# Decay products of the linear attention on GpSimd, and PSUM banks emptied ahead of the weight split in even slots

## The chip, the cores and the metric

One core of one Trainium2 chip runs the whole program in one launch. The metric is device microseconds (us), median over the runs; the kernel before was run three times.

## The reference, cut to what matters

Two blocks of a model run one after the other on 256 tokens of width 1024, all in float32. The change lies in the second block, which has two layers. Each layer is a feed-forward, a token mixer with two branches, and a feed-forward. The branches are a sparse attention of 8 heads and a gated linear attention (4 heads, key width 128, value width 256). Of the linear attention this is computed:

```python
q_dec = qc * jnp.exp(b)
k_intra = kc * jnp.exp(-b)
k_state = kc * jnp.exp(b_last - b)
A = jnp.where(causal, jnp.einsum('bnihd,bnjhd->bnhij', q_dec, k_intra), 0.0)
o_intra = jnp.einsum('bnhij,bnjhv->bnihv', A, vc.astype(jnp.float32))
```

Here b is the running sum of the logarithm of a gate. The branches then go through two output products, each scaled by a sigmoid gate of a projection of the same input.

## The kernel before, in words

**Split products.** All large products are made in a format with fewer mantissa bits, so each weight chunk (128 x 2048 float32, a ring of 4 slots loaded from HBM by SyncE's queue) is split in two parts. ScalarE writes the high part of a chunk (`mix_split`, L1552 to L1563, two halves of 128 x 1024), VectorE the low part (`mix_low`, L2287 to L2295, two halves, each after ScalarE's half). TensorE then makes three matmuls of 512 columns for each 128 x 128 weight block. A ring slot comes free when TensorE has read it, and its load is issued then.

**The attention part of a layer.** `attention()` exists once for each engine (TensorE L1267, ScalarE L1907, VectorE L2807), and the engines keep step by semaphores alone. The sparse attention goes over four pairs of heads, j = 0 to 3. Round j has these steps:
- TensorE: scores of the pair (L1277 to L1284), then `side_pair` (L1162), the product of one half of a projection with its weights, 48 matmuls of 128x512 into the two banks `side`. Then the transposes of the probabilities (`turn`, L1294, L1296), a second `side_pair`, and the values (L1309 to L1315).
- VectorE: maxima of the pair (L2824, L2827), the probabilities' scale (L2834 to L2841), the slot `beside(2j)`, two PSUM copies of transposed probabilities for each head (`turned`, L2848 and L2849), the slot `beside(2j+1)`, and, once ScalarE has taken its high part, the low part of the output (`output_low`, L2934) ahead of the next maxima.
- ScalarE: exponentials of the pair (L1912), `beside(2j)`, its share of the copies (L1920, L1921), `beside(2j+1)`, and the high part of the output (L1925).

**The slots.** `beside(s)`, s = 0 to 7 (ScalarE L1966, VectorE L2908), carries the projections that are made beside the heads. In slot s, ScalarE splits the chunks 16+2s and 17+2s, which the *next* `side_pair` reads (the first in its first half, the second in its second half), and empties the two `side` banks that the *current* `side_pair` fills (`side_take`, L1885, recorded at L1890). Slots 0 and 1 carry the values, 2 and 3 the output gate (two copies from each bank), 4 and 5 the first merge gate, 6 and 7 the second. From slot 2 on, the taking of the second bank is followed by `sigmoid_rest` (L1946 to L1950): a logarithm and an exponential over 128x1024, each with its table load.

The linear attention's own steps stand in the same slots. VectorE does the absolute value in slot 0 (L2910), the running sums in slot 2 (`sums`, L2851 to L2858), the differences in slot 3 (L2865), the gate product in slot 4 (L2923, L2924). ScalarE forms the decays in slot 4 (`decays`, L1932 to L1940). In slot 5 VectorE multiplies decays with queries and keys (`operands`, L2868 to L2878: four products of 128x512, two of 128x1024) and clears the 128x2048 tile `PlL` of weights (L2928). In round 3 TensorE makes the far weights (`far_weights`, L1224) between the first `side_pair` and the transposes, in the same two `side` banks, and the near weights (`near_weights`, L1241) after the second `side_pair`. VectorE collects both into `PlL` (`collect_far` L2880, `collect_near` L2895).

**GpSimd** masks weights in the first block (L3106), issues a few DMAs (L3110 to L3119), and then waits for the end of the last layer's attention to issue one more (L3122). Its queue is in order.

Of the kernel before, what the change touches and what calls it, by code (L numbers as in the profile page):

```python
# [9 lines left out]
ALU = mybir.AluOpType  # L10
# [3 lines left out]
P = 128  # L14
# [18 lines left out]
def build(nc, t, out):  # L33
    ctx = ExitStack()
    with ctx:
# [3 lines left out]
        def sem(name):  # L39
            return ctx.enter_context(nc.semaphore(name))  # L40
# [311 lines left out]
        gl_d = sem("gla_differences")  # L352
        gl_e = sem("gla_decays")
        gl_g = sem("gla_operands")
        gl_o = sem("gla_values")
        rb_done = sem("gla_gate_done")
        rb_sig = sem("gla_gate_sigmoid")
# [1048 lines left out]
        def _(act):  # L1406
# [500 lines left out]
            def attention():  # L1907
# [58 lines left out]
                def beside(s):  # L1966
                    l = c.layer - 1
                    if s == 6:
                        act.wait_ge(rb_done, c.layer)
                    for i in range(2):  # L1970
                        n = 2 * (s % 2) + i
                        mix_split(l, 16 + 2 * s + i)
                        if s < 2:
                            values(n)
                        elif s < 4:
                            gate(n)
                        elif s < 6:
                            merge_gate_(n, y2, gm_sig)
                        else:
                            merge_gate_(n, r2, gm1_sig)  # L1980
                    if s == 1:
                        log_decays()
                    elif s == 4:
                        decays()
                    if s in (6, 7):
                        c.side += 2 if s == 6 else 1
# [107 lines left out]
        def _(dve):  # L2094
# [685 lines left out]
            def side_give(fn):  # L2780

                dve.wait_ge(side_full, c.side + 1)
                fn(side[c.side % 2]).then_inc(side_out[c.side % 2], 1)
                c.side += 1
# [22 lines left out]
            def attention(l):  # L2807
# [57 lines left out]
                        dve.tensor_tensor(out=o, in0=v.rearrange("p h (n w) -> p h n w", w=per), in1=ref,  # L2865
                                          op=ALU.subtract).then_inc(gl_d, 1)

                def operands():  # L2868
                    for u in range(2):
                        dve.wait_ge(gl_e, 3 * c.layer - 2 + u)  # L2870
                        for half, src in enumerate((khL, qhL)):
                            o, s_ = (v.rearrange("p h (n a b) -> p h n a b", a=2, b=P >> u)[:, :, :, half, :]
                                     for v in (dec[:, u, :, :], src))
                            ins = dve.tensor_tensor(out=o, in0=s_, in1=o, op=ALU.mult)
                        ins.then_inc(gl_g, 1)
                    dve.wait_ge(gl_e, 3 * c.layer)
                    dve.tensor_tensor(out=dek, in0=khL, in1=dek, op=ALU.mult)
                    dve.tensor_tensor(out=dec[:, 2, :, :], in0=qhL, in1=dec[:, 2, :, :], op=ALU.mult).then_inc(gl_g, 1)  # L2878

                def collect_far():  # L2880
                    def across(b):
                        return dve.tensor_copy(PlL[:, :, 0, P:S], b[:, :].rearrange("p (h b) -> p h b", b=P))

                    def within(b):
                        for st in range(2):
                            ins = dve.tensor_copy(PlL[0:64, :, st, st * P + 64:st * P + P],
                                                  b[0:64, st * S:(st + 1) * S].rearrange("p (h b) -> p h b", b=64))
                        return ins

                    side_give(across)  # L2890
                    side_give(within)
                    dve.wait_ge(side_out[(c.side - 1) % 2], (c.side - 1) // 2 + 1)
                    dve.wait_ge(side_out[c.side % 2], c.side // 2)
# [14 lines left out]
                def beside(s):  # L2908
# [8 lines left out]
                    if s == 2:  # L2917
                        sums()
                    elif s == 3:
                        differences()  # L2920
                    elif s == 4:
                        dve.wait_ge(rb_sig, 2 * c.layer)
                        step(dve.tensor_tensor(out=rx, in0=rx, in1=r2, op=ALU.mult))  # L2923
                        dve.tensor_tensor(out=rx, in0=rx, in1=gainC.unsqueeze(1).to_broadcast([P, 2, D]),  # L2924
                                          op=ALU.mult).then_inc(rb_done, 1)
                    elif s == 5:
                        operands()
                        step(dve.memset(PlL[:, :, :, :], 0.0))  # L2928
                    elif s == 7:
                        collect_near()  # L2930

# [165 lines left out]
        def _(gp):  # L3097
            c = Count()

            for h in range(H):  # L3100
                for d in range(2):
                    gp.wait_ge(p_done, 2 * h + d + 1)
                    for n in range(2):
# [2 lines left out]
                        ins = gp.affine_select(out=v, in_=v, compare_op=ALU.is_ge, fill=0.0, base=0,  # L3106
                                               pattern=[[sign, P]], channel_multiplier=-sign)
                    ins.then_inc(pm_done, 1)
            gp.wait_ge(resid, 12)
            gp.dma_start(gateB[:, 1, :], t["fgain"][0:1].to_broadcast([P, D])).then_inc(final_in, 16)  # L3110
            gp.dma_start(onehot, t["onehot"]).then_inc(bias_dma, 16)
# [6 lines left out]

            gp.dma_start(TB, bass.AP(t["scratch"].tensor, P - 1, [[H * RW - 1, P], [RW, H], [1, S]])).then_inc(  # L3119
                bias_done, 16)  # L3120
            gp.wait_ge(hn_out, 2)
            gp.dma_start(gainC, t["fgain"][1:2].to_broadcast([P, D])).then_inc(final_in, 16)  # L3122
            gp.wait_ge(stored, 64)
# [179 lines left out]
```

## Time and profile before

| | |
|---|---|
| median of 3 runs | 2425.76 us (2425.75 to 2430.88) |
| profiled execution, its own time | 2424.43 us |
| its span in the profile | 2422.7 us |
| TensorE busy, share of the span | 2351.5 us, 97% |
| VectorE / ScalarE / GpSimd busy | 1570.5 / 1162.6 / 13.0 us |
| mean granted TensorE clock | 0.994 of full |
| attention of the first layer of block two | about 1405 to 1529 us of the span |
| attention of the second layer | about 2041 to 2165 us of the span |

In a timeline row the first number is the start in us from the span's start, the second the time of the group in us; [x <- engine tile line] is how long the engine sat idle before it and who ended that.

### The profile page before, as it was taken

What the parts mean: (1) busy time and instruction counts of PE and PEld (TensorE: products, weight loads), DVE (VectorE), ACT (ScalarE), POOL (GpSimd) and SP (SyncE); (2) the same over time, 40 slices, a digit from 0 to 9 for tenths busy, and PEclk for the clock granted to TensorE, in tenths of its full rate; (3) what the DMA queues carried; (4) which work ended last, traced back from release to release, by engine and by line L of the source; (5) the groups of instructions that cost most, each with busy time, mean ns of one, the idle gap of its engine ahead of it and who ended that gap; (6) DMA issues with size and microseconds to landing.
All of it is one profiled execution on the core that took longest, in us unless ns stands there. A gap on an engine that the chain in (4) does not pass through costs nothing.

```text
span 2422.7 us, 33029 instructions
## 1 busy us (share of the span) xinstructions
PE 2351.5 (97%) x13342; PEld 1974.8 (82%) x13342; DVE 1570.5 (65%) x2355; ACT 1162.6 (48%) x1725; POOL 13.0 (1%) x43
## 2 busy tenths in 40 slices
PE   7999999999999999999999998999999999989998
PEld 4887787888888887888888887888888888878887
DVE  4686434656655686667766468676776665766766
ACT  4212323435533345445444478554454446874444
POOL 0000000000000000000000000000000000000000
PEclk9999999999999999999999999999999999999999
DMA  7467322323521224654455643345545555434553
GB/s 301 188 240 267 122 91 103 120 87 124 203 86 57 88 90 164 235 191 174 175 190 191 221 157 140 134 180 191 190 175 191 191 171 217 152 119 164 195 189 137
DMA packets 57920, 399.67 MB, mean 165 GB/s; under 512 B 7789, under 2 KB 8309, under 8 KB 10280
## 3 DMA queue, kind: packets, MB, share of 16 engines
q1 hardware_dynamic: 52704, 383.80, 43.4%
q10 hardware_dynamic: 4272, 10.08, 1.2%
q0 software_dynamic: 800, 3.73, 0.5%
q8 instruction: 106, 1.74, 0.3%
q14 instruction: 38, 0.31, 0.0%
HBM read 396.53 MB, written 2.63 MB: 165 GB/s over the span
## 4 chain that ended last, share of the span: by engine, by line
PE 85%; DVE 6%; ACT 6%; DMA 1%; issue 1%; SPq 0%; DVEq 0%; ACTq 0%
PE pair L506 80%; DMA ring<-in_stream 1%; DVE ring_parts L2294 1%; ACT mix_high L1562 1%; PE pair L901 1%; DVE ring_parts L2284 1%; ACT arena L1912 1%; PE pair L619 1%; PE pair L884 1%; PE pair L1039 1%; ACT ring_high L1549 1%; PE pair L1294 0%; PE pair L848 0%; DVE rows L2411 0%; DVE X L2417 0%
## 5 line engine op out<-in xcount | busy, mean ns | idle before, releaser
L506 PE MATMUL pair<-xT_parts,ring_high 128*128 128x512 f32 x2112 | 747.8, 395 | 4.2 <-DVE ring_parts L2284 1.1
L506 PE MATMUL pair<-xT_parts,ring_parts 128*128 128x256 f32 (+2 forms) x2448 | 694.6, 298 | 7.4 <-DVE ring_parts L2294 4.9
L2284 DVE TENSOR_TENSOR ring_parts<-ring,ring_high 128x2048 fp32r<-128x2048 f32 x194 | 444.1, 2292 | 142.1 <-ACT ring_high L1549 142.0
L506 PEld LDWEIGHTS pair<-xT_parts,ring_parts 128*128 128x128 f32 (+1 forms) x2448 | 461.5, 189 | 51.2 <-issue 12.1
L506 PEld LDWEIGHTS pair<-xT_parts,ring_high 128*128 128x128 f32 x2112 | 384.5, 188 | 81.8 <-DVE ring_parts L2284 2.7
L1549 ACT ACTIVATE ring_high<-ring 128x2048 fp32r<-128x2048 f32 x198 | 377.3, 1909 | 68.2 <-DMA ring<-in_stream 68.2
L2294 DVE TENSOR_TENSOR ring_parts<-ring,mix_high 128x1024 fp32r<-128x1024 f32 x144 | 168.5, 1219 | 77.6 <-ACT mix_high L1562 77.2
L1600 ACT ACTIVATE arena<-pair 128x512 f32<-128x512 f32 x110 | 65.5, 596 | 259.7 <-PE pair L506 259.6
L506 PE MATMUL pair<-ring_parts,xT_parts 128*128 128x512 f32 (+1 forms) x448 | 174.3, 389 | 0.2 <-DVE rows L2524 0.2
L1562 ACT ACTIVATE mix_high<-ring 128x1024 fp32r<-128x1024 f32 x144 | 143.1, 1047 | 61.6 <-DMA ring<-in_stream 57.7
L506 PE MATMUL pair<-ring_parts,g_high 128*128 128x512 f32 x440 | 171.8, 391 | 0.2 <-issue 0.2
L506 PE MATMUL pair<-ring_high,g_high 128*128 128x512 f32 x440 | 171.3, 389 | 0.0
L506 PE MATMUL pair<-ring_high,g_low 128*128 128x512 f32 x440 | 171.2, 389 | 0.0
L506 PE MATMUL pair<-mix_high,xT_parts 128*128 128x512 f32 (+1 forms) x576 | 171.0, 380 | 0.0
L2337 DVE TENSOR_TENSOR arena<-pair,arena 128x512 f32<-128x512 f32 x110 | 75.7, 689 | 96.6 <-ACT arena L1600 96.6
L506 PE MATMUL pair<-xT_low_parts,ring_high 128*128 128x512 f32 x352 | 137.0, 389 | 0.0
L1562 ACT ACTIVATE grid_weights<-ring 128x1024 fp32r<-128x1024 f32 x56 | 56.1, 1052 | 140.6 <-PE pair L506 127.8
L506 PEld LDWEIGHTS pair<-mix_high,xT_parts 128*128 128x128 f32 x576 | 106.3, 188 | 20.5
L1611 ACT ACTIVATE arena<-arena 128x256 f32<-128x256 f32 x110 | 46.0, 418 | 141.2 <-DVE arena L2345 123.2
L1593 ACT ACTIVATE arena<-pair 128x512 f32<-128x512 f32 x22 | 13.1, 598 | 187.4 <-PE pair L506 187.4
L506 PE MATMUL pair<-xT_parts,mix_high 128*128 128x256 f32 (+1 forms) x544 | 100.7, 287 | 0.0
L506 PEld LDWEIGHTS pair<-ring_parts,xT_parts 128*128 128x128 f32 x448 | 84.1, 188 | 19.1 <-issue 2.3
(417 smaller groups left out, 3908.2 us busy)
## 6 DMA issues: line engine op xcount, KB each, us to landing
ring<-in_stream SPq DMA_DIRECT2D x338, 1024.0 KB, 4.8
xn<-in_mods SPq DMA_DIRECT2D x14, 1024.0 KB, 4.9
arena<-in_mods SPq DMA_DIRECT2D x14, 1024.0 KB, 4.9
arena<-in_bT ACTq DMA_DIRECT2D x1, 1536.0 KB, 8.9
bias_scratch<-bias_row POOLq DMA_DIRECT2D x1, 1536.0 KB, 8.3
X<-in_x ACTq DMA_DIRECT2D x1, 1024.0 KB, 11.9
X<-in_ctx ACTq DMA_DIRECT2D x1, 1024.0 KB, 16.4
arena<-in_bT ACTq DMA_DIRECT2D x1, 1024.0 KB, 7.3
```

What stands on the lines that cost most here:

```text
L506: m = pe.matmul(o, l, r, start=start, stop=stop)
L619: m = pe.matmul(bank[k][:, t_ * P:(t_ + 1) * P], X[:, t_, k * P:(k + 1) * P], diag[:, t_, :], start=True, stop=True)
L884: pe.matmul(bank[n // 2][:, (n % 2) * S:(n % 2 + 1) * S], km[lo:lo + 64, h // 2, n * P:(n + 1) * P], qm[lo:lo + 64, h // 2, :], start=True ...
L901: m = pe.matmul(misc[d][:, tt * 129:(tt + 1) * 129], Pm[d][:, n, tt * P:(tt + 1) * P], va[:, n, h, :], start=n == keys[0], stop=n == keys[-1])
L1039: m = pe.matmul(acc[c.acc % 4][:, st * S:(st + 1) * S], KX[d][:, 1, hh, st * P:(st + 1) * P], QP[d][:, hh, :], start=d == 0, stop=d == 1)
L1549: act.activation(high[:, ch % SLOTS, :], ring[:, ch % SLOTS].rearrange("p a b -> p (a b)"), ACT.Copy).then_inc(high_ready, 1)
L1562: act.activation(mix_high(l, m)[:, half], ring[:, ch % SLOTS].rearrange("p a b -> p (a b)")[:, half], ACT.Copy).then_inc(mix_high_ready, 1)
L1600: act.activation(cross[:, f % 2, :, :], pair[f % 2][:, :, S:2 * S], ACT.Copy).then_inc(cross_done, 1)
L1611: act.activation(sil2[:, f % 2, :], both[:, f % 2, 0, :], ACT.Silu).then_inc(sil_done, 1)
L2284: dve.tensor_tensor(out=ring_r[:, slot].rearrange("p a b -> p (a b)"), in0=w, in1=high[:, slot, :], op=ALU.subtract).then_inc(low_ready, 1)
L2294: dve.tensor_tensor(out=ring_r[:, slot].rearrange("p a b -> p (a b)")[:, half], in0=w, in1=mix_high(l, m)[:, half], op=ALU.subtract).then_ ...
L2337: dve.tensor_tensor(out=both[:, f % 2, :, :], in0=pair[f % 2][:, :, 0:S], in1=cross[:, f % 2, :, :], op=ALU.add).then_inc(both_done, 1)
```

## The change

Three things change, in both layers. `operands` goes from VectorE's slot 5 to GpSimd, with the same waits on ScalarE's decays. The clearing of `PlL` goes with it, behind the wait for the last decays, and VectorE's `collect_far` waits for it by a new semaphore. In ScalarE's even slots the split of each of the two chunks comes after the taking of the bank of the same index, and so, in slots 2, 4 and 6, the second chunk's split comes after `sigmoid_rest` too. Odd slots stay as they were.

```diff
@@ ScalarE, beside(s) @@
                     for i in range(2):
                         n = 2 * (s % 2) + i
-                        mix_split(l, 16 + 2 * s + i)
+                        if s % 2:
+                            mix_split(l, 16 + 2 * s + i)
                         if s < 2:
                             values(n)
...
                         else:
                             merge_gate_(n, r2, gm1_sig)
+                        if s % 2 == 0:
+                            mix_split(l, 16 + 2 * s + i)
@@ VectorE @@
-                def operands():
...
+                    dve.wait_ge(far_clear, c.layer)
                     side_give(across)
...
-                    elif s == 5:
-                        operands()
-                        step(dve.memset(PlL[:, :, :, :], 0.0))
@@ GpSimd @@
+            def operands(l):
+
+                for u in range(2):
+                    gp.wait_ge(gl_e, 3 * l + u + 1)
+                    for half, src in enumerate((khL, qhL)):
+                        o, s_ = (v.rearrange("p h (n a b) -> p h n a b", a=2, b=P >> u)[:, :, :, half, :]
+                                 for v in (dec[:, u, :, :], src))
+                        ins = gp.tensor_tensor(out=o, in0=s_, in1=o, op=ALU.mult)
+                    ins.then_inc(gl_g, 1)
+                gp.wait_ge(gl_e, 3 * l + 3)
+                gp.memset(PlL[:, :, :, :], 0.0).then_inc(far_clear, 1)
+                gp.tensor_tensor(out=dek, in0=khL, in1=dek, op=ALU.mult)
+                gp.tensor_tensor(out=dec[:, 2, :, :], in0=qhL, in1=dec[:, 2, :, :], op=ALU.mult).then_inc(gl_g, 1)
...
                 bias_done, 16)
+            operands(0)
+            operands(1)
             gp.wait_ge(hn_out, 2)
```

## Rows read from the trace of the kernel before

**Rows 1.** Page, part 1: busy us (share of the span) x instructions.
```profile
PE 2351.5 (97%) x13342; PEld 1974.8 (82%) x13342; DVE 1570.5 (65%) x2355; ACT 1162.6 (48%) x1725; POOL 13.0 (1%) x43
```

**Rows 2.** Waits of TensorE: who for whom, us in total, times, longest.
```profile
PE pair L506 <- ACT arena L1890: 12.9, 4, 6.1
```

**Rows 3.** Timeline, TensorE, round 3 of the first layer.
```profile
1508.59 2.04 PE L506 MATMUL pair<-arena 128*128 128x128 f32 x8 [6.12 <-ACT arena L1890]
1510.96 1.94 PE L506 MATMUL pair<-arena 128*64 128x64 f32 x16 [0.33 <-ACT arena L1890]
...
1525.92 1.15 PE L506 MATMUL pair<-arena 128*64 128x64 f32 x32
```

**Rows 4.** Timeline, ScalarE, slot 6.
```profile
1501.31 0.40 ACT L1912 ACTIVATE arena<-arena 128x128 f32<-128x128 f32 x1 [4.76 <-DVE arena L2827]
...
1505.98 1.99 ACT L1562 ACTIVATE mix_high<-ring 128x1024 fp32r<-128x1024 f32 x2
1507.87 0.57 ACT L1890 ACTIVATE arena<-pair 128x512 f32<-128x512 f32 x1
```

**Rows 5.** Timeline, VectorE, end of slot 5.
```profile
1492.43 2.49 DVE L2874 TENSOR_TENSOR arena<-arena 128x512 f32<-128x512 f32 x4
...
1497.56 1.76 DVE L2928 MEMSET arena<- 128x2048 f32 x1 [0.38 <-issue]
1499.36 0.43 DVE L2934 TENSOR_TENSOR oaT_low<-pair,oaT_high 128x256 fp32r<-128x256 f32 x1
```

**Rows 6.** Timeline, ScalarE, slot 2: second split, sigmoid, then copies.
```profile
1445.00 2.00 ACT L1562 ACTIVATE mix_high<-ring 128x1024 fp32r<-128x1024 f32 x2
...
1447.98 1.28 ACT L1949 ACT_TABLE_LOAD   x1
...
1452.61 0.47 ACT L1920 ACTIVATE arena<-pair 128x384 f32<-128x384 f32 x1
```

**Rows 7.** Timeline, VectorE, slots 2 to 4.
```profile
1444.24 4.63 DVE L2294 TENSOR_TENSOR ring_parts<-ring,mix_high 128x1024 fp32r<-128x1024 f32 x4
1448.78 1.22 DVE L2853 SCALAR_TENSOR_TENSOR arena<-arena 128x1024 f32<-128x1024 f32 x1
...
1454.74 2.36 DVE L2294 TENSOR_TENSOR ring_parts<-ring,mix_high 128x1024 fp32r<-128x1024 f32 x2
...
1465.55 0.42 DVE L2934 TENSOR_TENSOR oaT_low<-pair,oaT_high 128x256 fp32r<-128x256 f32 x1 [1.17 <-ACT oaT_high L1925]
...
1478.80 2.29 DVE L2923 TENSOR_TENSOR gateB<-gateB,arena 128x2048 f32<-128x2048 f32 x1
```

**Rows 8.** Timeline, TensorE: start of a side product, and the values of two rounds.
```profile
1448.09 0.48 PE L506 MATMUL pair<-ring_parts,xT_parts 128*128 128x512 f32 x1
...
1459.16 1.08 PE L1309 MATMUL pair<-arena 128*64 128x256 f32 x8
...
1487.12 1.08 PE L1309 MATMUL pair<-arena 128*64 128x256 f32 x8
```

**Rows 9.** Timelines of GpSimd and VectorE in the first block, GpSimd's last DMA.
```profile
502.16 0.54 POOL L3106 TENSOR_SCALAR_AFFINE_SELECT arena<-arena 128x128 f32<-128x128 f32 x2 [0.59 <-DVE arena L2487]
...
2177.36 0.55 POOL L3122 DMA_DIRECT2D gateB<-in_fgain  x1 [1190.74 <-DVE xn L3019]
...
502.42 2.48 DVE L2294 TENSOR_TENSOR ring_parts<-ring,first_high 128x1024 fp32r<-128x1024 f32 x2 [0.33 <-ACT first_high L1562]
...
552.64 2.36 DVE L2294 TENSOR_TENSOR ring_parts<-ring,first_high 128x1024 fp32r<-128x1024 f32 x2 [0.45 <-ACT first_high L1562]
```

**Rows 10.** TensorE timeline (two stalls); then windows, PEclk the number ahead of DMA share.
```profile
705.45 0.74 PE L506 MATMUL pair<-arena 128*64 128x64 f32 x17 [1.88 <-DVE arena L2689]
...
1385.18 0.38 PE L506 MATMUL pair<-xT_parts,ring_parts 128*128 128x256 f32 x1 [1.40 <-DVE ring_parts L2294]
...
705.50:707.50 2.00, 2.00 (x69) 2.00 (x71) 1.58 (x2) 1.62 (x2) 0.00 (x0) 1.00 0.45 57
...
1388.50:1389.00 0.50, 0.50 (x4) 0.50 (x3) 0.50 (x2) 0.50 (x1) 0.00 (x0) 0.50 0.86 360
```

More of the change, by code:

```diff
@@ L354, in build @@
         gl_g = sem("gla_operands")
+        far_clear = sem("gla_weights_cleared")
         gl_o = sem("gla_values")
@@ L2866, in differences @@
                                           op=ALU.subtract).then_inc(gl_d, 1)
-                def operands():
[L2869 to L2878, printed above, removed]
                 def collect_far():
```

## The prediction

> **What bounds the kernel now.** The page first: TensorE is busy for 97% of the span [rows 1], so a change on the other engines can only pay where TensorE stands still. The waits of TensorE show one such place that this change touches: `L506 <- ACT L1890`, four waits, 12.9 us in all, the longest 6.1 [rows 2]. The timeline has two of them in round 3 of each layer: before the first far weights (6.12 us) and before the second (0.33 us) [rows 3]. The layers are alike to 0.1 us, so I work out the first and count it twice.
>
> TensorE waits there for a `side` bank that ScalarE empties at 1507.87, after a split that began at 1505.98 [rows 4]. ScalarE itself had stood idle for 4.76 us before its exponentials at 1501.31, waiting for VectorE's maxima [rows 4]. VectorE was late because the products and the clearing held it from 1492.43 to 1499.36, 6.93 us [rows 5]. So the chain is products, clearing, maxima, exponentials, split, bank, and both parts of the change aim at it.
>
> The gap has a second price. The far weights ran slowly, as at the half clock that [rows 10] show after another stall: the second group, 16 matmuls, took 1.94 us, while 32 of the same kind later took 1.15 us [rows 3]. At full clock 16 would take 0.6, so 1.3 us a layer could come back.
>
> **Part 1, VectorE's relief in slot 5.** 6.93 us of VectorE go away, but not all is gained: the next step, `output_low`, waits for ScalarE's high part, and ScalarE was busy until 1501.31 - 4.76 = 1496.55. From there VectorE needs 1.95 us for the low part and one head's maxima (1499.36 [rows 5] to 1501.31 [rows 4]), which sets the exponentials at 1498.5 instead of 1501.3: 2.8 us.
>
> **Part 2, slot 6.** The bank is taken where the split began, 1.89 us earlier [rows 4]; the second bank gains the same. Parts 1 and 2 at this place alone would be 4.7, and with the clock 6.0 us a layer.
>
> **Part 3, the same edit in slots 2 and 4.** The diff moves the second chunk's split behind `sigmoid_rest` as well. That takes from 1447.98 to 1452.61, 4.63 us [rows 6]. Slot 2, step by step. Before, the second split began at 1445.00 [rows 6]. Now ScalarE's exponentials end at 1442.15 (1445.00 less a split of 1.9 and a bank of 0.95), it waits 1.5 for TensorE to fill bank 0, takes it (1.0), splits (1.9), takes bank 1 (1.0) and does the sigmoid (4.65). The second chunk's first half is out at about 1453.15, its low part 1.15 later, at 1454.3. TensorE's next side product began at 1448.09 and reads that chunk 5.5 us later [rows 8], at 1453.6: it stalls 0.7. VectorE, in order, is done with the slot's low parts at 1455.5, not 1448.8 [rows 7]; the sums and PSUM copies queued behind took from 1448.78 to 1454.74 [rows 7], 5.8 without idle time, and follow to 1461.2. TensorE's values, at 1459.16 before [rows 8] and 1459.9 now, wait for those copies: 1.3 more. Slot 3's splits and differences are done 5.0 us later; 1.17 of it was idle there [rows 7], so the next maxima, and ScalarE's exponentials, start 3.9 us later.
>
> Slot 4 repeats this on top: TensorE loses 0.9 at the transposes and the chunk's first use, 1.0 at its second chunk, and 1.5 at the copies, since VectorE's gate product (twice 2.29) [rows 7] again stands between late low parts and copies (values at 1492.6; 1487.12 before [rows 8]). TensorE arrives at round 3 5.5 us late, which eats most of the 6.45 us gap. ScalarE's output part is 4.0 late, at 1500.2. By then VectorE, without the products, is through (1497.2) and waits, so the exponentials start at 1502.1 (before: 1501.3). Bank 1 is taken, by the new order, at 1509.8, where the second far product before began at 1510.96 [rows 3]. TensorE ends its side product at 1507.8, does the first far product at full clock, and the second is done at 1510.3 instead of 1512.3 by the same bookkeeping: a gain of 2.0 us a layer, 4.0 in all. Slot 0 costs nothing: VectorE's absolute value covers the later split. Slot 6's late second split is covered too: TensorE reads that chunk 5.5 us into a side product that starts at 1512.
>
> **Part 4, GpSimd's work.** No row shows its two-input product. From below I take VectorE's own rate (0.62 us for each of the four, 2.49 / 4 [rows 5]), from above twice the select's rate: 0.27 us for 128 columns [rows 9] gives 1.1 us for 512 columns and one input, 2.2 for two. I take 1.1 and, for 1024 columns, 2.2, nearer to the low end because part of a select is fixed cost. The clearing lies between VectorE's 1.76 [rows 5] and 16 selects, 4.3 us. The six products and the clearing then take 11 us from 1486.4 on: the first far product is fed at 1489 and needed at 1508, the near one at 1497 and 1524. At twice the durations this still holds, so GpSimd's speed is on no path, nor is the new wait of `collect_far`. Behind the waiting GpSimd stands one DMA, at 2177.36, which waits for the last attention anyway [rows 9]. SyncE's loads follow TensorE's reads as before.
>
> **What the products do to VectorE** is the open price. In the first block a VectorE subtraction of the chunk kind overlapped a GpSimd select once: the pair took 2.48 us against 2.36 elsewhere, 0.12 more for some 0.27 of GpSimd [rows 9]. Bounds: nothing, or all of GpSimd's time in turns. I take the row: VectorE loses 0.45 of GpSimd's busy time where both read two operands. The first four products (4.4 us) fall on the gate product and stretch it and what follows by 2.3 us. The copies and values come that much later, TensorE reaches the far weights at 1510.1, after ScalarE; of the gain of 2.0 only 0.7 is left.
>
> The stall at the copies is then 3.8 us. Short stalls can cost clock: one of 1.40 us at 1385.18 was followed by windows with a granted clock of 0.50, while one of 1.88 us at 705.45 was followed by 1.00 [rows 10]. The drop after the first lasted 3.5 us, so 1.75 us of work; I charge it once a layer. Result: -0.7 + 1.8 = +1.1 us a layer, +2.2 in all. Against the profiled execution (2424.43) that is 2426.6; the median shown is 1.3 above it, so 2428.0.
>
> **Rivals.**
> - **No contention** (the bound of nothing). -2.0 a layer, 2421.8; with a drop of the clock after the stalls of 1.3 to 1.5 us, near 2425. For it: a select is a poor stand-in, the overlap is one row. Against: the row is not zero. Chance 0.21.
> - **VectorE and GpSimd take turns by whole instructions** (slower). The gate product and slot 5's four low parts stand against the six products: while GpSimd reads two operands, a VectorE instruction of two SBUF operands does not run. Each such instruction waits for a product of 1.1 or 2.2 us: together 7.8 us by 1505, so maxima start 4.8 us after the no-contention schedule, ScalarE is last again, the gap opens by 2 us and the clock falls before the far weights (1.3). -2.0 + 4.8 + 1.3 = +4.1 a layer, 2434.0. It decides once VectorE loses more than about two thirds of GpSimd's time. For it: 0.12 us is all that the select's reading of 128 columns can hold. Against: the select's full 0.27 was not lost. Chance 0.31. The Trainium skill, page "SBUF — State Buffer", section "Who interferes with whom", says that a VectorE instruction with two SBUF inputs contends with a GpSimd instruction that reads SBUF, and that the pair of ports is locked for a whole instruction; by it the sum would be this one.
> - **The order costs nothing in slots 2 and 4**, and the full 6.0 us a layer come: 2413.8. That asks that TensorE not miss the late chunk halves, which its own rows contradict. Chance 0.11.
> - The forecast, stretched or not by the clock (-1 to +2.4 a layer: 2424 to 2430.6), has 0.37.
>
> **Numbers.** 0.2% is 4.9 us, about what a measurement of this kernel can tell from no change. Forecast and no contention lie within it, but for 0.05 of the latter's and 0.05 of the former's chance at either side. Faster 0.16, same 0.48, slower 0.36. The range leaves out the full gain and the upper part of the turns (GpSimd's products longer still): 2420 to 2437.
>
> **What would show it.** In the changed profile: idle before the first far weights down from 6.12 to under 1 us (turns: 2 or more); new TensorE waits on L2294 in slots 2 and 4 of 0.5 to 1 us and on the copies before L1309 of 1.3, then 1.5 to 4 us; the gate product L2923 and L2924 at 2.29 us (no contention), 3 or more (forecast), or stretched by whole products (turns); GpSimd's products at 1.1 and 2.2 us; granted clock under 1.00 after the copies' stall. If TensorE has no new waits before round 3, part 3 is wrong and the time is near 2414.

## The result and the profile after

The changed kernel takes 2433.99 us (median of 11 runs, 2429.52 to 2437.81), the kernel before beside it 2427.82 us (11 runs, 2425.75 to 2430.88). The ratio is 1.0025, 95% interval 1.0016 to 1.0033: slower by 6.2 us. The time lies in the forecast range, 6.0 us above the 2428.0 us forecast; 2.1 of these 6.0 us lie in the kernel before, which took 2425.76 us in the three runs that the forecast started from. So a forecast of +2.2 stands against a measured +6.2 us. The profiled execution took 2430.51 us, span 2428.2, and is the second fastest of the eleven, so its trace shows less than the median loses.

The engines' busy times, page part 1, answer to [rows 1]:

```profile
PE 2355.7 (97%) x13342; PEld 1975.1 (81%) x13342; DVE 1566.1 (64%) x2341; ACT 1163.9 (48%) x1725; POOL 54.0 (2%) x57
```

VectorE lost 14 instructions but only 4.4 us, though 6.93 us a layer of products and clearing had left it. GpSimd is busy 41.0 us longer, where 11 us a layer had been costed. A good part of both numbers is waiting for each other.

Waits of TensorE (who for whom, us in total, times, longest), then its timeline in the first layer. They answer to [rows 2, 3]:

```profile
PE pair L1310 <- DVE arena L2853: 9.3, 4, 3.4
...
PE pair L507 <- DVE ring_parts L2298: 8.9, 11, 1.4
```

```profile
1458.05 0.50 PE L507 MATMUL pair<-ring_parts,xT_parts 128*128 128x512 f32 x1 [1.07 <-DVE ring_parts L2298]
...
1465.05 1.08 PE L1310 MATMUL pair<-arena 128*64 128x256 f32 x8 [1.22 <-DVE arena L2853]
...
1481.62 0.88 PE L1295 MATMUL pair<-ident,arena 128*128 128x128 f32 x6 [0.32 <-DVE arena L2845]
...
1489.34 0.50 PE L507 MATMUL pair<-ring_parts,xT_parts 128*128 128x512 f32 x1 [0.80 <-DVE ring_parts L2298]
...
1498.51 1.97 PE L1310 MATMUL pair<-arena 128*64 128x256 f32 x8 [3.43 <-DVE arena L2853]
...
1516.86 2.13 PE L507 MATMUL pair<-arena 128*128 128x128 f32 x24
```

The wait for `side` banks, 12.9 us before, is gone: the far weights start without idle time, all 24 matmuls in 2.13 us. In its place stand the five waits for VectorE shown above, in slots 2 and 4. They add up to 6.84 us in this layer, where before there were 6.45. Idle time was moved, not removed. The values at 1498.51 took 1.97 us where the same eight matmuls took 1.08 before [rows 8]: they ran at the lower clock.

Time, busy time and clock by round, TensorE first (PEclk is the number ahead of the DMA share). A round goes from the values of one pair to the values of the next. First the kernel before, first layer, rounds 1 to 3:

```profile
1431.21:1459.16 27.95, 27.95 (x157) 22.42 (x156) 21.69 (x68) 26.16 (x52) 0.00 (x0) 1.00 0.43 151
1459.16:1487.12 27.96, 27.96 (x158) 22.43 (x157) 22.80 (x64) 25.86 (x53) 0.00 (x0) 1.00 0.40 151
1487.12:1526.90 39.78, 33.34 (x214) 27.16 (x214) 30.15 (x75) 29.87 (x56) 0.00 (x0) 0.91 0.29 106
```

Then the changed kernel, with round 0 ahead:

```profile
1405.53:1434.40 28.87, 28.87 (x136) 23.97 (x137) 20.44 (x65) 15.32 (x40) 0.00 (x0) 0.88 0.40 146
1434.40:1465.05 30.65, 28.36 (x157) 22.38 (x157) 19.11 (x66) 27.59 (x54) 0.00 (x0) 1.00 0.38 138
1465.05:1498.51 33.46, 28.79 (x157) 22.39 (x157) 27.62 (x67) 28.75 (x56) 8.41 (x4) 1.00 0.35 126
1498.51:1532.71 34.20, 34.20 (x212) 27.19 (x214) 25.00 (x68) 25.96 (x51) 11.98 (x4) 0.90 0.33 124
```

Rounds 1 and 2 are 2.70 and 5.50 us longer, round 3 is 5.58 us shorter. Of the 8.20 us only 6.96 are idle time. The other 1.24 us stand in TensorE's busy time at a clock of 1.00 (28.36 + 28.79 against 27.95 + 27.96); by an estimate from these numbers each of the five stalls costs a further 0.25 us beyond its idle time. Round 0 is no part of the change: its 28.87 against 25.8 us elsewhere is a drop of the clock that falls there in some executions of several of these kernels. I therefore read rounds 1 to 3 alone, both layers together: 191.1 us before, 195.0 after, +4.0. This sum is the yardstick below.

VectorE in the changed kernel, from slot 4's low parts to the maxima, answers to [rows 5, 7]:

```profile
1488.07 2.36 DVE L2298 TENSOR_TENSOR ring_parts<-ring,mix_high 128x1024 fp32r<-128x1024 f32 x2 [4.23 <-ACT mix_high L1563]
1490.34 3.39 DVE L2916 TENSOR_TENSOR gateB<-gateB,arena 128x2048 f32<-128x2048 f32 x1
1493.77 3.28 DVE L2917 TENSOR_TENSOR gateB<-gateB 128x2048 f32<-128x2048 f32 x1
...
1498.29 4.61 DVE L2298 TENSOR_TENSOR ring_parts<-ring,mix_high 128x1024 fp32r<-128x1024 f32 x4
1503.80 0.42 DVE L2924 TENSOR_TENSOR oaT_low<-pair,oaT_high 128x256 fp32r<-128x256 f32 x1 [0.90 <-ACT oaT_high L1926]
...
1507.24 0.92 DVE L2831 TENSOR_SCALAR arena<-arena 128x6 f32<-128x6 f32 x1
```

GpSimd in the same stretch, and the eight 128x512 products by themselves (ns, least, median, greatest):

```profile
1490.10 13.93 POOL L3107 TENSOR_TENSOR arena<-arena 128x512 f32<-128x512 f32 x4 [501.53 <-ACT arena L1938]
1503.98 1.80 POOL L3110 MEMSET arena<- 128x2048 f32 x1
1505.74 2.39 POOL L3111 TENSOR_TENSOR arena<-arena 128x1024 f32<-128x1024 f32 x1
```

```profile
L3107 POOL TENSOR_TENSOR arena<-arena x8: 1477/3330/5911, 1490.1 to 2134.9; 128x512 f32<-128x512 f32 x8
```

The gate product was 2.29 and is 3.39 and 3.28. The four small products are 1.48, 3.34, 3.32 and 5.90 us long in order. The lengths fit VectorE and GpSimd waiting for each other's whole instructions: the first gate instruction has 1.10 us more in its record, the time until the first product was over, and the second product waited for it (3.34 = some 2.1 of waiting and 1.2 of work). The fourth product then waited for all of slot 5's low parts, which were themselves not stretched (4.61 for four). The clearing takes 1.80 to 1.82 us in all these kernels.

### The profile page after: what moved, and what is told of

It reads as the page before. It is cut to its first block, busy times and chain, and to the rows that moved or that the text cites. A ratio compares the mean times of both kernels' runs of the same rounds, so it can differ in the third digit from the quotient of the medians.

```text
span 2428.2 us, 33029 instructions
## 1 busy us (share of the span) xinstructions
PE 2355.7 (97%) x13342; PEld 1975.1 (81%) x13342; DVE 1566.1 (64%) x2341; ACT 1163.9 (48%) x1725; POOL 54.0 (2%) x57
## 4 chain that ended last, share of the span: by engine, by line
PE 85%; DVE 7%; ACT 5%; DMA 2%; issue 1%; SPq 0%; DVEq 0%; ACTq 0%
PE pair L507 80%; DVE ring_parts L2298 2%; DMA ring<-in_stream 2%; DVE ring_parts L2288 1%; PE pair L902 1%; ACT mix_high L1563 1%; ACT ring_high L1550 1%; PE pair L885 1%; PE pair L1040 1%; ACT arena L1913 0%; DVE rows L2415 0%; PE pair L620 0%; DVE X L2421 0%; PE pair L849 0%; PE pair L1280 0%
## 6 DMA issues: line engine op xcount, KB each, us to landing
X<-in_x ACTq DMA_DIRECT2D x1, 1024.0 KB, 12.1
```

## The experiments

Theory A: the late split behind `sigmoid_rest` in slots 2 and 4 costs more than the rest of the change gains, and contention of GpSimd with VectorE and the clock after the long stall are smaller terms on top. The rivals: GpSimd's contention is the loss; or the order's loss is small and the gain never was there. The table sums up all kernels. "Rounds" is the yardstick against the kernel before (191.1), "idle" TensorE's idle time in rounds 1 to 3 of the first layer (window less busy time), "work" its busy time in round 3 there.

| kernel | median, us | its kernel before | ratio, 95% interval | rounds, us | idle, us | work in round 3 |
|---|---|---|---|---|---|---|
| before | | | | 0 | 6.4 | 33.3 |
| the change | 2433.99 | 2427.82 | 1.0016 to 1.0033 | +4.0 | 7.0 | 34.2 |
| e1_gp_only | 2424.20 | 2428.81 | 0.9975 to 0.9994 | -2.8 | 4.2 | 34.2 |
| e2_order_only | 2434.59 | 2428.81 | 1.0014 to 1.0033 | +9.6 | 9.4 | 34.0 |
| e3_gp_slot6 | 2422.92 | 2428.81 | 0.9966 to 0.9988 | -5.1 | 3.0 | 34.0 |
| e4_split_before_sigmoid | 2424.45 | 2428.81 | 0.9978 to 0.9996 | -5.4 | 2.9 | 32.6 |
| e5_near_on_vector | 2421.67 | 2428.69 | 0.9959 to 0.9981 | -8.1 | 2.7 | 32.8 |
| e11_near_again (same) | 2421.58 | 2429.01 | 0.9956 to 0.9981 | -8.4 | 2.7 | 32.7 |
| e6_clear_and_slot6 | 2423.65 | 2428.69 | 0.9970 to 0.9988 | -4.6 | 3.3 | 34.1 |
| e7_after_gate_first | 2428.98 | 2428.69 | 0.9991 to 1.0010 | -0.2 | 6.9 | 31.3 |
| e8_low_parts_apart | 2434.46, one run | 2428.69 | | +5.7 | 7.1 | 32.7 |
| e9_slot6_only | 2428.58 | 2429.01 | 0.9990 to 1.0007 | -2.3 | 4.6 | 34.3 |
| e12_slot6_again (same) | 2424.77 | 2428.01 | 0.9981 to 0.9998 | -2.1 | 4.6 | 33.9 |
| e10_after_low_parts | 2423.66 | 2429.01 | 0.9973 to 0.9991 | -5.6 | 3.0 | 32.8 |

The yardstick comes from one execution each and agrees with the difference of the medians within 2.2 us, except for e2 (3.8 us), whose profiled execution was itself 4.5 us above its median.

**GpSimd's part alone** (all of the change but ScalarE's order):

```diff
@@ ScalarE, beside(s): as before the change @@
-                        if s % 2:
-                            mix_split(l, 16 + 2 * s + i)
+                        mix_split(l, 16 + 2 * s + i)
...
-                        if s % 2 == 0:
-                            mix_split(l, 16 + 2 * s + i)
```

> GpSimd forms the products and clears the weights; ScalarE's slots are as in the kernel before. Theory A (the order in slots 2 and 4 is what costs; GpSimd's share of the contention is small): no TensorE wait in slots 2 and 4, the wait before the first far weights falls from 6.1 to about 3 us, the way from a layer's first scores to its last values is about 117 us (before: 121.5 and 121.2), the time is 7 to 9 us below the kernel before. Theory B (GpSimd beside VectorE is what costs): the gate product L2916 and L2917 stays stretched and VectorE is late, the time is above that of the kernel before by 2 us or more.

**The order alone** (the four lines above as in the change; products and clearing stay on VectorE):

```diff
@@ VectorE, against the change @@
+                def operands():
...
-                    dve.wait_ge(far_clear, c.layer)
...
+                    elif s == 5:
+                        operands()
+                        step(dve.memset(PlL[:, :, :, :], 0.0))
@@ GpSimd @@
...
-            operands(0)
-            operands(1)
```

> ScalarE's even slots take the banks first, as in the changed kernel; products and clearing stay on VectorE. Theory A: TensorE waits about 0.7 to 1.1 us at the late chunk halves and 1.3 to 1.5 us at the copies in slots 2 and 4, and since VectorE's 6.9 us come on top, the wait before the far weights is still 3 us or more: 122 to 125 us from scores to last values, time 3 to 8 us above the kernel before. Theory B: the order costs nothing and saves up to 2 us a layer: time 2 to 6 us below the kernel before.

Measured: the first 4.6 us faster than before, less than the 7 to 9 expected; the second 5.8 us slower, as expected. TensorE's two stalls in round 3 with GpSimd's part alone, and VectorE's slot 5:

```profile
1511.66 2.05 PE L507 MATMUL pair<-arena 128*128 128x128 f32 x8 [3.90 <-ACT arena L1891]
1514.04 1.94 PE L507 MATMUL pair<-arena 128*64 128x64 f32 x16 [0.33 <-ACT arena L1891]
```

```profile
1493.07 9.45 DVE L2295 TENSOR_TENSOR ring_parts<-ring,mix_high 128x1024 fp32r<-128x1024 f32 x4 [3.05 <-ACT mix_high L1563]
```

TensorE with the order alone, slot 4:

```profile
1492.59 0.50 PE L506 MATMUL pair<-ring_parts,xT_parts 128*128 128x512 f32 x1 [0.79 <-DVE ring_parts L2297]
...
1499.67 1.08 PE L1309 MATMUL pair<-arena 128*64 128x256 f32 x8 [1.34 <-DVE arena L2852]
```

The whole loss of the change is there without GpSimd, and the new stalls 1.07, 1.27, 0.31 and 0.79 are those of the changed kernel to 0.05 us. The last one, before the values, is 1.34 without GpSimd and 3.43 with it. GpSimd's part alone is a gain, but VectorE's slot 5 shows its price: the four low parts take 9.45 us instead of 4.6, since here they meet the 128x1024 products. So the gap closes by 2.2 us, not by 2.8.

**The order in slot 6 only, and the split ahead of the sigmoid.**

```diff
@@ e3_gp_slot6, against the change @@
-                        if s % 2:
+                        if s != 6:
                             mix_split(l, 16 + 2 * s + i)
...
-                        if s % 2 == 0:
+                        if s == 6:
                             mix_split(l, 16 + 2 * s + i)
@@ e4_split_before_sigmoid: all even slots, but inside the taking of the bank @@
                     side_take((dst[:, t_, g * N:(g + 1) * N], lambda b: b[:, :], ACT.Exp, -1.0))
+                    if split_m is not None:
+                        mix_split(c.layer - 1, split_m)
                     if t_:
...
```

> The changed kernel, but the bank is taken ahead of the split in slot 6 alone; slots 0, 2 and 4 have the old order. Theory A: no waits in slots 2 and 4, the wait before the first far weights about 1 us and before the second about 1.5 us, 114.5 us from scores to last values, time 11 to 14 us below the kernel before. Theory B: as the changed kernel, 4 us or more above the kernel before.

> The changed kernel, but in the even slots the second chunk's split stands between the taking of the second bank and the logarithm and exponential of the sigmoid. Theory A, which lays the cost on the split that waits 4.6 us behind the sigmoid and not on the bank being taken first: TensorE has no waits in slots 2 and 4, about 1.5 us are left before each far product, 115.2 us from scores to last values, time 10 to 13 us below the kernel before. Rival to it: taking the banks first costs by itself (a split 1 us later is late enough): time at or above the kernel before.

Measured: 5.9 and 4.4 us faster than before. Almost no waits are left in slots 2 and 4, as expected, but the gains expected, 11 to 14 and 10 to 13 us, were about twice as large or more. Round 3 still runs in part at the lower clock (0.91 in e3; 0.95 and 0.91 in e4). TensorE in e3:

```profile
1507.72 1.34 PE L507 MATMUL pair<-arena 128*128 128x128 f32 x8 [1.99 <-ACT arena L1891]
1510.10 1.94 PE L507 MATMUL pair<-arena 128*64 128x64 f32 x16 [1.04 <-ACT arena L1891]
```

The change differs from e3 in slots 0, 2 and 4 of ScalarE's order alone, and is 12.1 us slower (+6.2 against -5.9, each to its own kernel before). e4 says that it is not the early bank that costs but the 4.6 us of sigmoid between the bank and the second split: with the split ahead of it, the stalls of slots 2 and 4 fall from 6.84 to 0.2 us and the gain stands.

**Which part of GpSimd's work gains.**

```diff
@@ e5_near_on_vector, against e3: the two 128x1024 products stay on VectorE @@
...
+                    elif s == 5:
+                        dve.wait_ge(gl_e, 3 * c.layer)
+                        dve.tensor_tensor(out=dek, in0=khL, in1=dek, op=ALU.mult)
+                        dve.tensor_tensor(out=dec[:, 2, :, :], in0=qhL, in1=dec[:, 2, :, :], op=ALU.mult).then_inc(gl_n, 1)
...
@@ e6_clear_and_slot6, against e3: GpSimd only clears, VectorE's operands() as before @@
...
             def operands(l):
-                for u in range(2):
...
                 gp.wait_ge(gl_e, 3 * l + 3)
                 gp.memset(PlL[:, :, :, :], 0.0).then_inc(far_clear, 1)
-                gp.tensor_tensor(out=dek, in0=khL, in1=dek, op=ALU.mult)
...
@@ e10_after_low_parts, against e3 @@
             def operands(l):
+                gp.wait_ge(mix_low_ready, 2 * split_before(l, 27) + 2)
```

> GpSimd forms only the four products of 128x512 and clears the far weights; the two products of 128x1024 stay on VectorE at the end of slot 5, as before; ScalarE's early take of the first bank stands in slot 6 alone (as in e3). Theory A (the two products of 128x1024 on GpSimd take turns with slot 5's low parts and stretch them to 9.4 us, and this delays the maxima and the exponentials of slot 6): slot 5's four low parts together fall to 4.6 to 5.1 us, TensorE's idle time before the first far weights falls from 1.99 to about 1.0 us, and the time lies 1 to 2 us under e3, so 7 to 9 us under the kernel before. Rival (the stretch of the low parts lies beside other work, and what the products cost on VectorE comes back): the same as e3 within 1 us, with the gap before the first far weights at 2 us or more.

> All six decay products stay on VectorE; GpSimd only clears the far weights (1.8 us); ScalarE's early take of the first bank stands in slot 6 alone. Theory A (the move of the products to GpSimd is worth almost nothing net: it frees 5 us of VectorE and gives most of it back in stretched low parts): as fast as e3 within 2 us, 5 to 8 us under the kernel before, with slot 5's low parts at 4.6 to 5.1 us and no stretch of the gate product. Rival (the products' move is what gained in e1 and e3): 3 us or more above e3, so at most 3 us under the kernel before, with a gap of 3 us or more before the first far weights.

> As e3 (products and clearing on GpSimd, ScalarE's order changed in slot 6 alone), but GpSimd starts only when VectorE has finished slot 5's low parts. Theory A (GpSimd's products cost VectorE only where its instructions read two operands from SBUF, and only these turns stretch it): slot 5's four low parts take 4.6 to 5.1 us, the products of 128x512 about 1.3 us each, TensorE's gap before the first far weights is 1.0 to 1.6 us, and the time equals that of e5 (7 us under the kernel before) within 2 us. Rival (the later start makes the products themselves late, or they take turns with the maxima as well): the far product waits for the products or the maxima are 2 us or more late, and the time is at or above that of e3 (6 us under the kernel before).

> The same kernel as e5_near_on_vector, beside the two others of this group. If its lead over e3 and e6 was more than the drops of the clock that wander between executions, it is again 6 to 8 us under the kernel before and 1 to 3 us under the other two here.

Measured: e5 and its repeat e11 7.0 and 7.4 us faster than before, e6 5.0, e10 5.4. The gap before the far weights in e5 is 1.48 us where about 1.0 was expected. Against the kernels measured beside it, e11 is 2.1 us under e10 and 7.0 under e9_slot6_only (below). TensorE and VectorE in e5:

```profile
1509.77 1.13 PE L508 MATMUL pair<-arena 128*128 128x128 f32 x8 [1.48 <-ACT arena L1892]
1512.15 1.94 PE L508 MATMUL pair<-arena 128*64 128x64 f32 x16 [1.25 <-ACT arena L1892]
```

```profile
1493.62 5.03 DVE L2299 TENSOR_TENSOR ring_parts<-ring,mix_high 128x1024 fp32r<-128x1024 f32 x4 [3.06 <-ACT mix_high L1564]
```

VectorE in e10, where GpSimd's clearing and its products of 128x1024 meet the maxima, then GpSimd, ScalarE and TensorE there:

```profile
1501.84 1.08 DVE L2831 TENSOR_SCALAR arena<-arena 128x6 f32<-128x6 f32 x1
...
1503.33 1.96 DVE L2831 TENSOR_SCALAR arena<-arena 128x6 f32<-128x6 f32 x1
...
1505.44 2.16 DVE L2838 TENSOR_SCALAR arena<-arena 128x6 f32<-128x6 f32 x1 [0.15 <-ACT arena L1913]
```

```profile
1501.09 1.81 POOL L3111 MEMSET arena<- 128x2048 f32 x1
1502.86 2.39 POOL L3112 TENSOR_TENSOR arena<-arena 128x1024 f32<-128x1024 f32 x1
1505.21 2.36 POOL L3113 TENSOR_TENSOR arena<-arena 128x1024 f32<-128x1024 f32 x1
```

```profile
1502.96 0.41 ACT L1913 ACTIVATE arena<-arena 128x128 f32<-128x128 f32 x1 [2.90 <-DVE arena L2831]
```

```profile
1508.38 1.79 PE L507 MATMUL pair<-arena 128*128 128x128 f32 x8 [2.43 <-ACT arena L1891]
```

Clearing plus slot 6 (e6) gets 5.0 of e3's 5.9 us; all six products on GpSimd add nothing that these runs can tell from zero. The four small ones alone (e5) add about 2 us to e6 by the medians, 3.5 by the yardstick: they fit into the time that VectorE waits for slot 5's splits. Most of that is clock: in the first layer e5 has 0.5 us less idle time than e6 and 1.3 us less work in round 3. The large ones beside the low parts stretch these (e3).

Behind the low parts (e10) the low parts are whole (4.74 us), yet e10 is no better than e3, as its rival said. What costs there, by the trace, is the clearing. The first `TENSOR_SCALAR` of the maxima, 0.17 us otherwise, took 1.08 and ended at 1502.92, as GpSimd's clearing did at 1502.90; ScalarE's exponentials waited for it. Counted from the values before, they start 0.93 us later than in e5, and the gap before the far weights is 0.95 us longer (2.43 against 1.48). The second layer is alike (1.06 us, end 2133.20; clearing until 2133.17). The two large products stretch two more of these instructions, to 1.96 and 2.16 us, but ScalarE has no idle time before the second head's exponentials and TensorE no wait for what follows. I had expected turns neither for an instruction with one tile as input nor beside one that only writes. Large products behind the low parts with the clearing out of the maxima's way were not run. The version that beats both kernels is e5.

**Slot 6 alone**, and once more:

```diff
@@ e9_slot6_only, e12_slot6_again: against the kernel before @@
-                        mix_split(l, 16 + 2 * s + i)
+                        if s != 6:
+                            mix_split(l, 16 + 2 * s + i)
...
+                        if s == 6:
+                            mix_split(l, 16 + 2 * s + i)
```

> Only ScalarE's order in slot 6 is changed; products and clearing stay on VectorE, slots 0, 2 and 4 as before. The bank is taken a split (1.9 us) earlier and nothing else moves. Theory A (slot 6 is the gain of the order, slots 2 and 4 its loss): TensorE's gap before the first far weights falls from 6.12 to about 4.2 us, 2 us a layer, so 3 to 5 us under the kernel before; the clearing, in comparison with the kernel that has both, is then worth another 1 to 4 us. Rival (the far product is fed by something else too): no more than 1 us under the kernel before.

> The same kernel as e9_slot6_only. There the gap before the first far weights shrank by 1.86 us a layer as expected, yet the time fell by only 0.4 us. If that was where the drops of the clock happened to fall in that set of runs, this set is 2 to 4 us under the kernel before. If the shorter gap is really given back (the clock still falls before the far weights and takes as much as before), it is again within 1.5 us of it.

Measured: 0.4 us faster, then 3.2 us. The gap and the round in e9:

```profile
1511.08 2.05 PE L506 MATMUL pair<-arena 128*128 128x128 f32 x8 [4.26 <-ACT arena L1890]
```

```profile
1491.47:1530.31 38.84, 34.25 (x214) 27.96 (x215) 29.97 (x75) 29.93 (x56) 0.00 (x0) 0.91 0.30 109
```

The gap shrank from 6.12 to 4.26, 1.86 us, exactly the split that was stepped over. The round shrank by only 0.94 (39.78 to 38.84), because its work grew from 33.34 to 34.25 us. The granted clock of the round is 0.91 in both, 3.5 us of clock lost (38.84 x 0.09). Before, part of the slow stretch lay inside the gap, where nothing runs: the clock was down from 1506.6 to 1513.5 us, 2.0 us of it before the matmuls began at 1508.59. In e9 it was down from 1510.5 to 1517.7, only 0.6 us of it before 1511.08, so more of it lies on matmuls. Half of the shorter gap is given back. The two sets of runs, on two chips, are compatible with the yardstick's -2.2 us, and neither settles it alone. The first set fits the rival (at most 1 us), the second the expectation of 2 to 4 us.

**The long stall before the values.**

```diff
@@ e7_after_gate_first, against the change @@
             def operands(l):
+                gp.wait_ge(rb_done, l + 1)
@@ e8_low_parts_apart, against the change: VectorE, mix_low @@
+                    if l >= 0 and m in (26, 27):
+                        dve.wait_ge(mix_low_ready, 2 * split_before(l, m) + n + 1)
```

> The changed kernel, with GpSimd's products waiting until VectorE has finished the gate product. Theory A (the stall of 3.43 us before the values is 2.1 us of turns taken by the gate product with GpSimd's products, on top of 1.3 us that the late split costs): the gate product's two instructions fall from 3.39 and 3.28 to 2.29 us each, the stall before the values to 1.3 to 1.5 us; the products then take turns with slot 5's low parts or maxima instead, so that the time is 0 to 4 us under the changed kernel. Rival (the stall has another cause, the late split alone): the stall stays above 3 us.

> The changed kernel, with VectorE waiting for its own completion between slot 5's four low-part instructions, so that they aren't queued back to back. Theory A (GpSimd's fourth product waited 4.6 us because VectorE went from one low part straight to the next and never let go): the fourth product falls from 5.9 us to 2.5 us or less, and the four low parts stretch from 4.6 us to 7 to 10 us. Rival (the fourth product is slow for a reason of its own): it stays at 5.9 us and the low parts take 4.8 us or less.

Measured: e7 is 2428.98 us, 0.3 above its kernel before and, each to its own kernel before, 5.9 below the change, more than I had expected. VectorE and the rounds 2 and 3 of TensorE:

```profile
1494.03 2.29 DVE L2916 TENSOR_TENSOR gateB<-gateB,arena 128x2048 f32<-128x2048 f32 x1
1496.35 2.29 DVE L2917 TENSOR_TENSOR gateB<-gateB 128x2048 f32<-128x2048 f32 x1
...
1499.89 7.87 DVE L2298 TENSOR_TENSOR ring_parts<-ring,mix_high 128x1024 fp32r<-128x1024 f32 x4
```

```profile
1468.73:1500.11 31.38, 28.86 (x157) 22.39 (x157) 25.54 (x67) 26.62 (x54) 1.38 (x2) 1.00 0.37 134
1500.11:1533.49 33.38, 31.34 (x212) 25.35 (x214) 28.37 (x68) 27.83 (x53) 13.03 (x6) 1.00 0.35 127
```

The gate product is whole again and the stall before the values is 1.30 us. But the low parts pay instead (7.87), the banks are late by 0.80 and 1.25 us, and the idle time of the layer is the same as in the change: 6.9 against 7.0 us. What differs is the clock. In the change round 3's work is 34.20 us at a clock of 0.90, here it is 31.34 at 1.00. The same idle time in stalls of at most 1.3 us left the clock alone; with one stall of 3.43 us the work took 2.9 us longer in the first layer, 1.3 us in the second (32.62). The same stall in e8 cost 1.4 us of work in the first layer (32.69) and 4.4 in the second (35.77, clock 0.86), so what it costs differs from pass to pass.

The 128x512 products and VectorE's low parts in e8:

```profile
L3109 POOL TENSOR_TENSOR arena<-arena x8: 1480/2908/3345, 1492.4 to 2135.7; 128x512 f32<-128x512 f32 x8
```

```profile
1500.59 7.99 DVE L2298 TENSOR_TENSOR ring_parts<-ring,mix_high 128x1024 fp32r<-128x1024 f32 x4
```

With a pause between the low parts the longest product falls from 5.9 to 3.3 us (the fourth to 2.5) and the low parts stretch from 4.61 to 7.99 us, as theory A has it: in the change GpSimd was kept out by VectorE's unbroken row. But a row without a pause isn't enough to keep it out. In e7 VectorE's low parts have none, and they alternate with the products all the same (each 2.3 us, product and low part). Who gets the turn at the border between two instructions stays open.

## Why the prediction was right or wrong

**What bounds, and parts 1 and 2.** The chain was right. Part 2, 1.89 us, measured 1.86 (e9). Part 1, 2.8 us, measured 2.2 in e1, because there the large products stretch slot 5's low parts, which the step did not have in it. "Parts 1 and 2 at this place alone", 6.0 a layer, is too much: e3, which is just that, gained 5.9 us in both layers together, 3.0 a layer. Of the 6.0, 4.7 were idle time: e3 has 3.4 less of it (6.44 to 3.03), for the stretched low parts and a second bank that comes 1.04 us late instead of 0.33. The other 1.3 were clock that was to come back and did not: in e3 the second group still took 1.94 us, and the work of round 3 grew by 0.6 us (34.0 against 33.3). "At full clock 16 would take 0.6" was wrong too: e7 shows 16 in 1.12 us at a clock of 1.00, the price of 32 in [rows 3]; such short matmuls don't scale with their number. 24 in one row took 2.13.

**Part 3** was the step that carried the sign, and it held. Forecast 0.7 and 1.3 us of stalls in slot 2: measured 1.07 and 1.22. Slot 4: 0.9 and 1.0 forecast, 0.32 and 0.80 measured. At the copies 1.5 without contention: 1.34 (e2) and 1.30 (e7). TensorE was to reach round 3 5.5 us late and was 6.1 late without contention (rounds 1 and 2 of e7: 30.66 + 31.38 against 27.95 + 27.96), 8.2 late in the change, where 5.5 + 2.3 = 7.8 had been forecast. The stalls of e7 add up to only 4.7 of the 6.1; the rest stands in TensorE's busy time at full clock, a cost of a stall that no step of the sum has. Slot 0's order cost nothing: round 0 is 25.8 us in both wherever its clock is 1.00.

**Part 4.** GpSimd's small product, forecast 1.1, is 1.27 us undisturbed, the large one 2.39 (2.2), the clearing 1.80 (1.76 as the lower end). None of them, nor the wait of `collect_far`, shows up in TensorE's waits.

**Contention.** The size was right and the mechanism wrong. I had VectorE lose 0.45 of GpSimd's time, 2.3 us on the gate product (0.45 of the 4.4 us is 2.0; the sum used 2.3); it lost 2.09 (3.39 + 3.28 - 2 x 2.29), but by whole instructions, two turns of about a product each. This is what the Trainium skill says, page "SBUF — State Buffer", section "Who interferes with whom", and the trace agrees: 3.39 against 2.29. The rival of turns had this mechanism and priced it at 4.8 us a layer, since it let slot 5's low parts lose as well. In the change they lost nothing (4.61 us for four), GpSimd lost instead. Its 2434.0 us is close to the measured 2433.99, but not by its own path: no gap opened before the far weights, and the low parts kept their pace.

**The clock was the term that was mis-sized.** The forecast charged 1.75 us a layer for the stall at the copies, from the drop behind one earlier stall. The four passes that have the 3.43 us stall (the change and e8, two layers each) took 2.9, 1.3, 1.4 and 4.4 us more work in round 3 than e7's 31.34: 2.5 on the mean. Removing only that stall's long form (e7) took 5.9 us off, 2.9 a layer, at the same idle time. With 2.5 to 2.9 for 1.75 and 8.2 for 7.8 us of lateness the forecast becomes +2.25 to +2.65 a layer, +4.5 to +5.3 in all, against +6.2 measured. The rest is less than these runs resolve: the interval of the ratio is 3.9 to 8.0 us.

**What hitting the range is worth.** The range was 17 us wide and held two of the rivals too, so the time alone proves none of this. By the prediction's own line of 0.2%, 4.9 us, the change is slower, to which it gave 0.36, and not the same, to which it gave 0.48. The sum came out too low by 4 us, because the clock after the long stall and the lateness were both priced too low.

**The rivals.** "No contention" would have given 2421.8, 4.0 under the kernel before. e7 takes the contention off the gate product and comes to 2429.0, 0.3 above it, though its products meet the low parts instead, so the pure case was not run. "The order costs nothing" fell with e2: the order alone is 5.8 us slower. Of the signs named ahead, the idle time before the far weights (under 1 us: 0), the new waits (0.5 to 1, then 1.3, then 1.5 to 4: 1.07, 0.80, 1.22, 3.43), the gate product (3 or more: 3.39, 3.28) and a clock under 1.00 behind the copies' stall (the windows' 0.90) all came.

## What to carry to other kernels

When a change moves one engine's step ahead of another, price what it is moved *past* for every slot that the edit touches: here one slot gained 1.9 us of gap and two others lost 6 us of lateness, and limiting the edit to slot 6 turned +6.2 into -5.9 us. Add up TensorE's idle time over a whole layer before and after, since stalls wander, and look separately at the clock: the same 7 us of idle time in pieces of at most 1.3 us cost less than with one piece of 3.4. When work is given to GpSimd, put its two-input products where VectorE waits anyway, and leave on VectorE those that don't fit there. An instruction that only writes, such as clearing, did no harm beside VectorE's two-input work, but it held up a small one-input instruction on which ScalarE waited (e10).

## What the runs showed of the hardware that was not expected

- A shorter gap need not return its whole length: with 3.5 us of clock lost in the round either way, 1.86 us less idle time came with 0.91 us more work.
- TensorE's granted clock falls to 0.50 of full (1.2 GHz of 2.4) in drops that take 1.7, 3.4 or, in e8's second layer, 5.1 us of full clock away, and some of them fall in one execution and not in the next at code that is the same: round 0 took 28.9 us (clock 0.88) or 25.8 (1.00). The same kernel had one of these drops in round 0 of the second layer in e9 and none in e12. Runs of one kernel spread over 5 to 14 us, so a difference of 2 us needed the yardstick beside the medians (e9 and e12).
- A VectorE `TENSOR_SCALAR` over 128x6 takes 0.17 us without GpSimd beside it. Wherever one met a GpSimd instruction (the change, e7, e8, e10), it ended 0.02 to 0.04 us after that instruction: 0.92 and 1.04 us beside products in the change, up to 2.16 in e10, and 1.08 and 1.06 us beside the clearing in e10. The maxima's custom instructions beside a product kept their 0.28 and 0.41 us in the change. The Trainium skill, page "SBUF — State Buffer", section "Who interferes with whom", has it that such instructions contend when they run in a mode that takes both ports; no run here shows the mode.
- The clearing (GpSimd writes only) left VectorE's two-input low part beside it in e3 at 1.21 us, its undisturbed time. With the `TENSOR_SCALAR` above, this makes it matter which VectorE instruction meets it.
